# First loads of x in three pieces, and the turning and rounding of those pieces between the first weight units, in a transformer trunk on one core

## The reference

```python
def swiglu(x, w13, w2):
    gate, up = jnp.split(x @ w13, 2, axis=-1)
    return (jax.nn.silu(gate) * up) @ w2

for l in range(DEPTH):
    x = layer_norm(ALPHA * x + 0.5 * swiglu(x, ffn1_w13[l], ffn1_w2[l]), ln_g[l, 0], ln_b[l, 0])
    ...
```

## Time and profile before

| what | value |
|---|---|
| median of 3 runs | 1113.51 us (1113.4 to 1114.01) |
| the profiled execution, its own time | 1113.61 us |
| span of that execution in the trace | 1111.4 us |
| TensorE busy | 1100.4 us, 99% of the span |
| VectorE busy | 687.1 us, 62% |
| ScalarE busy | 532.4 us, 48% |
| GpSimd busy | 79.5 us, 7% |
| DMA | 203.16 MB, mean 183 GB/s |

### The profile page before, as it was taken

One profiled execution on the slowest core, in us unless ns is written; L12 is line 12 of the kernel. 1 busy time (PEld: TensorE's weight loads), 2 busy tenths in 40 slices (PEclk: granted clock), 3 DMA queues, 4 the chain that ended last, 5 costly groups with the idle time before them and its releaser, 6 DMA issues.

```text
span 1111.4 us, 16288 instructions
## 1 busy us (share of the span) xinstructions
PE 1100.4 (99%) x5868; PEld 948.9 (85%) x5868; DVE 687.1 (62%) x876; ACT 532.4 (48%) x729; POOL 79.5 (7%) x120
## 2 busy tenths in 40 slices
PE   9999999999999999999999999999999999999997
PEld 7888888999999888888888888889999988888885
DVE  4755555887765765555585555558977766555554
ACT  4644444556454554444454444445664646444442
POOL 0270000140100100000010000001401000000000
PEclk9999999999999999999999999999999999999999
DMA  8766566354664476666567665654546556666651
GB/s 291 234 216 189 180 190 205 120 163 160 195 203 152 162 239 192 184 188 191 168 197 220 189 189 188 189 162 123 166 148 203 187 156 208 190 189 188 190 170 38
DMA packets 156801, 203.16 MB, mean 183 GB/s; under 512 B 12656, under 2 KB 137840, under 8 KB 156752
## 3 DMA queue, kind: packets, MB, share of 16 engines
q1 hardware_dynamic: 153696, 193.51, 55.7%
q0 software_dynamic: 2912, 8.92, 2.5%
q10 hardware_dynamic: 144, 0.07, 0.0%
HBM read 201.41 MB, written 1.05 MB: 182 GB/s over the span
## 4 chain that ended last, share of the span: by engine, by line
PE 96%; DVE 2%; issue 0%; DMA 0%; ACT 0%; POOL 0%; POOLq 0%; DVEq 0%; ACTq 0%
PE ps L581 92%; PE ps L822 2%; PE ps L664 2%; DVE w_lo L1387 1%; DMA x<-in_x 0%; DVE tmp L1485 0%; PE ps L1050 0%; DVE xT L1420 0%; DVE x L1474 0%; DVE xT L1398 0%; PE ps L903 0%; PE ps L956 0%; DVE x L1498 0%; PE ps L1008 0%; PE ps L1010 0%
## 5 line engine op out<-in xcount | busy, mean ns | idle before, releaser
L1387 DVE TENSOR_TENSOR w_lo<-raw,w_hi 128x1024 fp32r<-128x1024 f32 (+1 forms) x247 | 300.3, 1222 | 163.7 <-ACT w_hi L1145 162.5
L1145 ACT CAST w_hi<-raw 128x1024 fp32r<-128x1024 f32 (+1 forms) x247 | 256.2, 1046 | 182.9 <-PE ps L581 142.6
L581 PE MATMUL ps<-w_hi,xT 128*128 128x512 f32 (+1 forms) x912 | 292.0, 393 | 0.8 <-DVE xT L1420 0.7
L581 PEld LDWEIGHTS ps<-w_hi,xT 128*128 128x128 f32 x912 | 171.0, 188 | 35.8 <-DVE xT L1420 1.5
L581 PE MATMUL ps<-w_hi,mixT 128*128 128x512 f32 x688 | 198.0, 390 | 0.0
L581 PE MATMUL ps<-v_flat,xT 128*128 128x512 f32 (+1 forms) x660 | 178.3, 391 | 0.0
L581 PE MATMUL ps<-w_lo,xT 128*128 128x512 f32 (+1 forms) x456 | 175.7, 389 | 0.0
L1145 ACT CAST v_flat<-raw 128x1024 fp32r<-128x1024 f32 (+1 forms) x114 | 118.8, 1046 | 86.9 <-PE ps L581 77.7
L581 PEld LDWEIGHTS ps<-w_hi,mixT 128*128 128x128 f32 x688 | 128.8, 188 | 26.4
L581 PEld LDWEIGHTS ps<-v_flat,xT 128*128 128x128 f32 x660 | 123.1, 188 | 25.0 <-DVE cqp L1387 0.2
L581 PE MATMUL ps<-w_lo,mixT 128*128 128x512 f32 x344 | 109.9, 389 | 0.0
(11 more groups left out here) (164 smaller groups left out, 1280.5 us busy)
## 6 DMA issues: line engine op xcount, KB each, us to landing
raw<-in_ffn_w SPq DMA_DIRECT2D x352, 256.0 KB, 3.2
raw<-in_ffn_w SPq DMA_DIRECT2D x88, 512.0 KB, 3.6
raw<-in_mem_wkv SPq DMA_DIRECT2D x32, 512.0 KB, 4.5
raw<-in_w_out SPq DMA_DIRECT2D x16, 512.0 KB, 4.5
raw<-in_mem_wq SPq DMA_DIRECT2D x16, 512.0 KB, 5.6
raw<-in_mem_wo SPq DMA_DIRECT2D x16, 512.0 KB, 4.8
gb<-in_ln_g POOLq DMA_DIRECT2D x8, 512.0 KB, 4.6
gb<-in_ln_b POOLq DMA_DIRECT2D x8, 512.0 KB, 5.8
```

The source lines that it names most:

```text
L581: return nc.tensor.matmul(dst, stand, move, start=start, stop=stop, skip_group_check=True)
L1145: nc.scalar.copy(slot_hi[slot[n]][:, 0:size], raw[:, n % RAW, 0:size]).then_inc(hi_done, 1)
L1387: nc.vector.tensor_tensor(slot_lo[slot[n]][:, s], raw[:, n % RAW, s], slot_hi[slot[n]][:, s].bitcast(F32), ALU.subtract).then_inc(lo_done, 1)
```

## The change

x's eight tiles of a row are taken in three pieces, `FIRST_TILES`: tiles 0 and 1, tiles 2 and 3, tiles 4 to 7. SyncE loads piece 0 of block 0 (128 KB); piece 0 of block 1 (128 KB) is issued from ScalarE's queue behind the identity; pieces 1 (256 KB) and 2 (512 KB) come for both blocks in one load each, behind units 0 and 1. The turns and roundings go by these pieces. In unit 0 the two blocks' products for tile 0 come first, then both blocks' for tile 1. TensorE turns piece 1 after unit 0 and piece 2 after unit 1. ScalarE's and VectorE's lists become: piece 0 of each block with a half of unit 0 behind it, piece 1 of both, unit 1, piece 2 of both, then `ffn`. The first activation on ScalarE (which brings its table) reads a zeroed tile instead of the identity.

```diff
@@ plan_ffn
-            marks = [[("turned", b, 0)] for b in range(TB)] + [UNIT_] + [[("turned", b, 1)] for b in range(TB)]
-            marks += [UNIT_] * 2 + [["U", "I", "I"]]
+            marks = []
+            for part in range(3):
+                marks += [[("turned", b, part)] for b in range(TB)] + ([UNIT_] if part < 2 else [])
+            marks += [UNIT_, ["U", "I", "I"]]
...
+        FIRST_TILES = [(0, 2), (2, 4), (4, KT)]
+        def first_turned(b, part):
+            k = FIRST_TILES[part][1] - FIRST_TILES[part][0]
+            return ps[:, 4 + 2 * b + part % 2, 0:k * P].rearrange("p (k s) -> p k s", s=P)
@@ block.sync
-            def load_x(b, c):
-                cols = slice(c * D // 2, (c + 1) * D // 2)
-                sp.dma_start(x[:, b, cols], a["x"][0, b * P:(b + 1) * P, cols]).then_inc(x_landed[b][c], 16)
-            load_x(0, 0)
+            def load_x(part):
+                cols = slice(FIRST_TILES[part][0] * P, FIRST_TILES[part][1] * P)
+                sp.dma_start(x[:, :, cols], a["x"][0].rearrange("(b p) d -> p b d", p=P)[:, :, cols])\
+                    .then_inc(x_landed[part], 16)
+            sp.dma_start(x[:, 0, 0:2 * P], a["x"][0, 0:P, 0:2 * P]).then_inc(x_landed[0][0], 16)
...
-                        if n == 0:
-                            load_x(1, 0)
-                        if n == 1:
-                            for b in range(TB):
-                                load_x(b, 1)
+                        if n < 2:
+                            load_x(n + 1)
@@ block.tensor, up_first
                     first_turn(0, 0)
                     warm(4)
                     pe.wait_ge(turned_lo[0], turned_lo_value(0, 0))
                     pe.wait_ge(first_hi, 1)
                     both(0, 0, 0)
+                    pe.wait_ge(x_landed[0][1], 16)
+                    first_turn(1, 0)
                     pe.wait_ge(first_lo, 1)
                     remainder(0, 0, 0)
-                    first_turn(1, 0)
+                    pe.wait_ge(turned_lo[1], turned_lo_value(1, 0))
+                    both(0, 1, 0)
+                    remainder(0, 1, 0)
                     pe.wait_ge(hi_done, 1)
-                    both(0, 0, 1)
+                    for b in range(TB):
+                        both(0, b, 1)
                     unit_split(u)
-                    remainder(0, 0, 1)
-                    pe.wait_ge(turned_lo[1], turned_lo_value(1, 0))
-                    for k in range(2):
-                        both(0, 1, k)
-                        last = remainder(0, 1, k)
+                    for b in range(TB):
+                        last = remainder(0, b, 1)
                     reach(last, ("unit", u))
-                    for b in range(TB):
-                        first_turn(b, 1)
+                    next_turns(1)
                     for j in range(1, 4):
                         pe.wait_ge(hi_done, j + 1)
...
+                        if j == 1:
+                            next_turns(2)
@@ block.scalar (block.vector alike)
             act.dma_start(cst[:, 0:P], consts[:, 0:P]).then_inc(ident_landed, 16)
-            act.wait_ge(ident_landed, 16)
-            ready_gate()
-            turn(0, xT, 0, [0])
-            ahead_to(1)
-            turn(1, xT, 1, [0])
+            act.dma_start(x[:, 1, 0:2 * P], a["x"][0, P:2 * P, 0:2 * P]).then_inc(x_landed[0][1], 16)
+            act.wait_ge(dve_step, 1)
+            nc.scalar.activation(st[:, 80:81], ev[:, 0, 0:1], ACT.Silu)
+            first_turn(0)
+            first_turn(1)
             ahead_to(2)
-            turn(0, xT, 0, [1])
-            turn(1, xT, 1, [1])
+            first_turn(2)
+            def first_turn(part):
+                for b in range(TB):
+                    act.wait_ge(pe_done, done["turned", b, part])
+                    nc.scalar.copy(xT[:, slice(*FIRST_TILES[part]), 0, b * P:(b + 1) * P], first_turned(b, part))\
+                        .then_inc(turned_hi, 1)
+                    if part == 0:
+                        first_half(b)
```

More of the change, by code:

```diff
@@ L746, in remainder, with first_turn, next_turns @@
                                        t == KT - 1)
-                    def first_turn(b, c):
-                        pe.wait_ge(x_landed[b][c], 16)
-                        turn_half(b, x[:, b, :], b, c)
+                    def first_turn(b, part):
+                        for i, k in enumerate(range(*FIRST_TILES[part])):
+                            last = nc.tensor.transpose(ps[:, 4 + 2 * b + part % 2, i * P:(i + 1) * P],
+                                                       x[:, b, k * P:(k + 1) * P], ident)
+                        reach(last, ("turned", b, part))
+                    def next_turns(part):
+                        pe.wait_ge(x_landed[part], 16)
+                        for b in range(TB):
+                            first_turn(b, part)
+                    pe.wait_ge(x_landed[0][0], 16)
                     first_turn(0, 0)
@@ L1096, in _, with look_ahead @@
             assert milestones[0] == len(plan.units_by)
-        def look_ahead(split):
-            state = dict(next=0)
+        def look_ahead(split, first):
+            state = dict(next=first)
             def ahead_to(limit):
@@ L1172, in ready_gate @@
             def ready_gate():
-                nc.scalar.activation(st[:, 80:81], ident[:, 0:1], ACT.Silu)
+                nc.scalar.activation(st[:, 80:81], cst[:, C_ID:C_ID + 1], ACT.Silu)
+            def first_turn(part):
+                for b in range(TB):
+                    act.wait_ge(pe_done, done["turned", b, part])
[3 more added lines that the diff above has]
+                        first_half(b)
             def turn(job, dst, b, halves=range(HALVES)):
```

46 lines of the change are left out of this document (24 added, 22 removed).

## The result

The changed kernel takes 1116.43 us (median of 10 runs, 1116.03 to 1116.96) against 1113.56 us for the kernel before on the same chip (10 runs, 1113.32 to 1114.02): a ratio of 1.0026, 95% interval 1.0018 to 1.0034, slower by 2.9 us. The forecast was 1116.5, slower. The profiled execution took 1116.24 us, with a span of 1114.3 us against 1111.4 before.

The account below looks back on a forecast made before the run. TensorE, busy 1089.62 of 1091.00 us, was taken as the bound, so unit 2's start sets the end: 1.0 us gained in unit 0, then 1.6 and 1.9 us idle put it at 17.7, +3.0, hence 1116.5 us; range 1115.5 to 1118.5.

Parts of the forecast that it names:

- The start: Up to unit 0's end: unit 0 begins at 6.0 instead of 6.65 us and ends at 10.1, 1.0 us ahead.
- Unit 1: Its rounding queues behind piece 1's on ScalarE: TensorE idles 1.6 us, unit 1 begins at 12.15 (11.87 before).
- Unit 2: Its rounding follows piece 2's transposes and roundings: another 1.9 us idle, unit 2 begins at 17.7 (14.70 before).
- The sum: Unit 2's start, 17.7 less 14.70, makes the whole run 3.0 us longer: 1116.5 us.
- The high bound: Unit 0 from 6.4 us and 0.3 us more in signals and roundings: +3.8 us.
- What was costed at nothing: Loads of x pieces 1 and 2, ScalarE's second queued load, later unit loads (unit 6 used 3.0 us later): no added wait.
- The other queue: Block 1's 128 KB from ScalarE's queue lands by 5.9 us at the slowest; activation table some 0.4 us later, costing nothing.
- The rival that the later slack swallows the delay: TensorE's 1.38 us idle after 12 us makes the late start good: +1.6 us, 1115.1, not slower; chance 0.07.
- The rival that ScalarE rounds ahead all the same: ScalarE rounds units ahead of the turns; unit 2 at 16.1, +1.4 us, 1114.9; chance 0.03.
- The rival of the clock: TensorE's clock falls in the new gaps; 4 us at half pace loses 2 us more, 1118.5; chance 0.10.

Follow-up runs that it names:

- e4: Kernel before, only with ScalarE and VectorE taking unit 1 behind the roundings of both second halves; 1115.38 us, ratio 1.0017.
- e2: Changed kernel, but TensorE turns piece 2 right behind piece 1, ahead of unit 1; 1114.07 us, ratio 1.0003 to the kernel before.
- e5: Changed kernel, but block 1's piece 0 is issued by SyncE behind unit 0 instead of from ScalarE's queue; 1116.30 us, ratio 1.0023.
- e3: Changed kernel with one more copy of unit 1 on ScalarE ahead of its rounding; 1119.21 us, median of five runs from 1117.13 to 1120.20.
- e1: Changed kernel, but ScalarE rounds unit 1 ahead of piece 1's roundings and unit 2 ahead of piece 2's; 1115.73 us, ratio 1.0021.
- e8: Changed kernel with two more copies of unit 1 on ScalarE ahead of its rounding; 1120.04 us, ratio 1.0063.
- e6: Changed kernel, but TensorE turns piece 1 in the middle of unit 0 and piece 2 in the middle of unit 1; 1113.18 us, ratio 0.9999.
- e10: e9 with unit 1 split by halves and piece 2's turns behind unit 1's w_hi matmuls; 1113.15 us, ratio 0.9995 to the kernel before.
- e11: e10 with piece 2's turns moved four matmuls forward, between unit 1's two halves; 1112.47 us, ratio 0.9989 to the kernel before.
- e7: e3 with ten warm-up products on TensorE ahead of unit 1's wait and six ahead of unit 2's; 1117.69 us, ratio 1.0035.
- e9: e6 with block 1's first turn right behind block 0's, ahead of the warm-up products; 1112.87 us, repeated at 1113.00, ratio 0.9994 both times.

## Why the prediction was right, point by point

- **The start.** The chain of steps was right, but two of its numbers are partly luck. Unit 0 at 6.0, measured 5.93. Block 1's x ready at 7.8, measured 7.77. Unit 0 done at 10.1, measured 9.95: the nine matmuls took 2.18 us, not 2.25. Rounding 256 columns 0.38 and 0.42, measured 0.37 and 0.42. One miss: the first turn began at 3.82, not 4.05. I had taken the end of the warm-up products' record, 3.99, for a floor, but records of matmuls overlap the next one's. A second miss made it good: from the start of the four warm-up products to unit 0 I counted 1.47 us, and it was 1.63 (4.30 to 5.93). And 9.95 is the earliest end of unit 0 of seven executions that begin alike; the others have 10.03 to 10.49.
- **Unit 1** at 12.15, measured 12.01, with 1.46 us idle by the bracket and 1.66 by starts, forecast 1.6. **Unit 2** at 17.7, measured 17.57, with 1.67 and 1.92, forecast 1.9. From 9.95 to 12.01 the chain took 2.06 (2.05 expected), from 14.86 to 17.57 it took 2.71 (2.71 expected). These were the terms that carry the sum, and e4 (such a wait alone in the kernel before, 1.91 us by starts, +1.75 in the median) and e2 (piece 2's turn back, -2.4) show what such a wait costs by itself.
- **The sum.** +3.0, measured +2.87. Taking the delay of unit 2 for that of the whole run left out two small terms of opposite sign: unit 2 itself takes 0.13 us longer behind transposes, and the run's time beyond the span is 0.3 us shorter. That they nearly cancel is luck. The high bound, too, adds up to +3.7 (0.4 and 0.3 on top of 3.0) and not +3.8. The size otherwise comes out of one reading that was right: not how long each step takes, but what stands behind what on ScalarE once the transposes have no matmuls beside them.
- **What was costed at nothing.** The loads of x: no wait on them. Unit 6 was used at 30.68, 3.0 us later than in the earlier trace rows, with no wait. The other queue: nothing. I had taken 4.7 us as the slowest case for that load; it took 2.8 in the changed kernel and 3.6 from SyncE's queue (e5), where 4.7 would have held up block 1's turn.
- **The rival that the later slack swallows the delay** fell: 1.38 us idle before, 1.37 after 20 us now, and TensorE is 3.00 us late at unit 3 and 2.92 at its last matmul. In e3's profiled run the added 1.31 us at unit 2 arrived as 1.32.
- **The rival that ScalarE rounds ahead all the same** fell with the timeline; e1 put this order in by hand. For the changed kernel's unit 2 it would have meant 16.1; by hand it came at 16.69.
- **The rival of the clock** didn't come about in the changed kernel. Its mechanism is real: the rows of e8 show it behind 3.35 us of idle time, and the mean clock was 0.997 or less in all five of its runs. With 2.4 us three of five runs had a low mean clock and a longer time (e3), and so had one or two of 11 in kernels with idle times about 1 us or less (e1, e6); there the fall is read from the mean clock and the time, not seen in a trace. A mean of 0.997 alone is no proof: the kernel before has runs at 0.997 that took 1113.50 and 1113.41. Its price, put at 2 us, was 1.6 in the profile, and e3's slower runs took 1.7 to 2.6 us more than its profiled one. So 0.10 was a fair chance, and the argument against it (the only fall in the trace before came 4.5 us after the last matmul) was weaker than I took it to be: in e8 it fell at about 14.3 us, 3.6 us after the last transpose had ended at 10.76.

## What to carry to other kernels

When an engine's list is written by hand, ask of each step that is moved which later step now queues behind it, and whether TensorE still has work for as long as the chain behind it takes; here 2.7 us pass from piece 2's first transpose to the end of the unit's rounding behind it, and TensorE had only the 0.8 us of transposes to do meanwhile; eight matmuls more fill it (e6), four don't (e10). Cutting loads and roundings finer won 1.1 us in the first 10 us of the profiled pair and lost 3.6 in the two waits behind them (by starts), with 0.4 for four transposes that moved behind unit 0: 2.9 in all. The same pieces, turned in the middle of the units, with block 1's first turn early and unit 1 split in halves (e11), end 1.2 us below the kernel before. A stretch without slack (TensorE busy for 99.9% of it) passes a change in its start through one to one, so that the forecast can be made for one point in time. That point is best put where the pace is the old one again (unit 3 here, 3.00 us late), and what a run's time holds beyond the span can move too (0.3 us here).

## What the runs showed of the hardware that I had not expected

- The pace of the first microseconds differs from run to run of the same instructions. Four warm-up products (eight records) took 1.79 us in the changed kernel, 1.30 in e3, 1.06 in e8 and 1.91 in e7, as TensorE came up to its full clock sooner or later: two records took 0.49 us in the first six products (2.93 us for twelve records) and 0.24 in e7's later ones (2.40 for twenty). A quick start of the clock didn't bring unit 0 forward: in e3 and e8 its first matmul, at 6.27 and 6.14, waited 0.76 and 0.92 us for the rounding of the first half of weights, whose load was there by 5.51 and 5.38 instead of 5.17, and in e1 it began at 5.83, but at half the pace.
- The granted clock may fall with little idle time: one of 11 runs of e6, whose profiled run has no single idle time above 0.7 us after 6 us, took 1115.25 us at a mean of 0.996. That run was not the profiled one, so neither the fall nor its stretch is shown.
- Filling an idle time on TensorE with products that nobody reads (e7) went with a median of 1117.69 us instead of e3's 1119.21, with no shorter chain: unit 2 began at 18.77, and at 18.88 in e3's profiled run. The two were timed on different chips, five runs each.
- The landing of one load moved by more than 1 us between two executions of the same instructions (unit 1 at 9.05 in e9 and 10.20 in its repeat), and the whole run moved with it.
